# The front of an encoder layer: modulation quarters, norms and two weight tiles interleaved part by part

## What is computed

```python
mod = silu(c) @ w_mod + b_mod                      # shift1, scale1, gate1, shift2, scale2, gate2
h = rms_norm(x, g_mix) * (1 + scale1) + shift1
z = h @ w_in                                       # u_f | u_r | u_g
y_f = fourier_mixer(u_f, w_fourier)
y_r = bidirectional_rglru(conv(u_r), ...) * gelu(u_g)
x = x + gate1 * (concat(y_f, y_r) @ w_out)
x = x + gate2 * (square(relu(h2 @ w_ff1)) @ w_ff2)  # h2 from x as h above, with shift2, scale2
return rms_norm(x, g_final)
```

## Time and profile before

| | us |
|---|---|
| median of 3 runs | 1533.9 |
| the three runs | 1526.1, 1533.9, 1630.98 |
| the profiled execution, as timed | 1533.22 |
| its span in the trace | 1531.4 |
| PE busy in that span | 1433.7 |
| n = 5 (end of weight tile 1) done | 107.07 |
| n = 35 (end of the weight tiles) done | about 325.6 |

### The profile page before, as it was taken

One profiled execution on the slowest core, in us unless ns is written; L12 is line 12 of the kernel. 1 busy time (PEld: TensorE's weight loads), 2 busy tenths in 40 slices (PEclk: granted clock), 3 DMA queues, 4 the chain that ended last, 5 costly groups with the idle time before them and its releaser, 6 DMA issues.

```text
span 1531.4 us, 18516 instructions
## 1 busy us (share of the span) xinstructions
PE 1433.7 (94%) x7584; PEld 1203.2 (79%) x7584; DVE 830.9 (54%) x766; ACT 572.9 (37%) x664; POOL 558.4 (36%) x308
## 2 busy tenths in 40 slices
PE   3899999999899758999999999998999999999995
PEld 1467777788688548888888888887888888888884
DVE  6747778764344995534543443462565343344554
ACT  5447878445232342222232232232232322333230
POOL 5431212117200886454545545542232232232220
PEclk9899999999999888999999999999999999999997
DMA  9232322202512113332343333349998443445532
GB/s 381 98 118 102 143 88 73 83 9 78 189 55 83 48 49 124 132 148 110 121 165 114 121 151 121 117 167 388 386 382 308 162 181 138 145 189 203 193 124 83
DMA packets 74515, 232.35 MB, mean 152 GB/s; under 512 B 5568, under 2 KB 9792, under 8 KB 65728
## 3 DMA queue, kind: packets, MB, share of 16 engines
q1 hardware_dynamic: 74432, 231.17, 40.6%
HBM read 166.14 MB, written 65.01 MB: 151 GB/s over the span
## 4 chain that ended last, share of the span: by engine, by line
PE 58%; DVE 3%; DMA 1%; issue 1%; ACT 0%; SPq 0%; DVEq 0%; ACTq 0%
PE bank L887 19%; PE bank L888 19%; PE bank L889 19%; DMA hin<-hid_all 1%; DVE hin_lo L1876 0%; DVE x L1916 0%; DVE hid L1840 0%; DMA w_raw<-in_w_ff 0%; PE bank L946 0%; PE bank L939 0%; DVE fin_acc L1900 0%; DVE t4b_s L1774 0%; DVE lo_r L1782 0%; ACT hin_hi L1363 0%; DVE hid L1850 0%
## 5 line engine op out<-in xcount | busy, mean ns | idle before, releaser
L887 PE MATMUL bank<-hin_hi,w_lo 128*128 128x256 f32 (+1 forms) x896 | 303.1, 338 | 4.3 <-DVE hin_lo L1876 4.3
L888 PE MATMUL bank<-hin_lo,w_hi 128*128 128x256 f32 (+1 forms) x896 | 302.8, 338 | 0.0
L889 PE MATMUL bank<-hin_hi,w_hi 128*128 128x256 f32 (+1 forms) x896 | 302.2, 337 | 0.0
L1876 DVE TENSOR_TENSOR hin_lo<-hin,hin_hi 128x3072 fp32r<-128x3072 f32 x28 | 140.4, 5016 | 214.6 <-ACT hin_hi L1363 214.6
L2095 POOL TENSOR_TENSOR w_lo<-w_raw,w_hi 128x2048 fp32r<-128x2048 f32 x28 | 130.9, 4674 | 335.8 <-ACT w_hi L1351 334.3
L887 PEld LDWEIGHTS bank<-hin_hi,w_lo 128*128 128x128 f32 x896 | 170.9, 191 | 23.1 <-issue 4.7
L889 PEld LDWEIGHTS bank<-hin_hi,w_hi 128*128 128x128 f32 x896 | 170.6, 190 | 18.2
L888 PEld LDWEIGHTS bank<-hin_lo,w_hi 128*128 128x128 f32 x896 | 170.9, 191 | 17.6
L1351 ACT ACTIVATE w_hi<-w_raw 128x2048 fp32r<-128x2048 f32 x28 | 53.7, 1917 | 297.5 <-PE bank L889 175.8
L887 PE MATMUL bank<-t_hi,w_lo 128*128 128x512 f32 (+1 forms) x320 | 114.1, 357 | 14.5 <-ACT hid L1308 11.7
L1308 ACT ACTIVATE hid<-bank 128x768 f32<-128x768 f32 (+2 forms) x68 | 52.6, 773 | 182.8 <-PE bank L889 173.9
(11 more groups left out here) (258 smaller groups left out, 3270.2 us busy)
## 6 DMA issues: line engine op xcount, KB each, us to landing
hin<-hid_all SPq DMA_DIRECT2D x28, 1536.0 KB, 6.6
hid_all<-hid SPq DMA_DIRECT2D x105, 384.0 KB, 2.3
w_raw<-in_w_ff SPq DMA_DIRECT2D x36, 1024.0 KB, 9.0
w_raw<-in_w_ff SPq DMA_DIRECT2D x68, 256.0 KB, 2.9
mod_raw<-in_w_mod SPq DMA_DIRECT2D x16, 1024.0 KB, 6.5
x<-in_xT SPq DMA_DIRECT2D x6, 2048.0 KB, 13.1
mod_first<-in_w_mod SPq DMA_DIRECT2D x4, 2048.0 KB, 21.6
w_sums<-w_raw SPq DMA_DIRECT2D x8, 1024.0 KB, 14.4
```

The lines of the kernel that those rows point to most:

```text
L887: pe.matmul(out, w_lo, v_hi, start=first, stop=False, skip_group_check=True)
L888: pe.matmul(out, w_hi, v_lo, start=False, stop=False, skip_group_check=True)
L889: return pe.matmul(out, w_hi, v_hi, start=False, stop=last, skip_group_check=True)
L1876: dve.tensor_tensor(hin_lo[n % 3][:].rearrange("p t n -> p (t n)"), hin[n % 3][:].rearrange("p t n -> p (t n)"), hin_hi[n % 3][:].rearrang ...
```

## The change

The front is written out part by part. A part (c, q) is column group c with the row tiles 2q and 2q + 1; `FRONT` lists the twelve. In each part PE multiplies **both** weight tiles 0 and 1, into six banks. The norms of c = 1 and 2 and the quarters 1 to 3 are placed between parts. The loads go in that order too: x in six halves, weight tile 0, quarter 0 (in four pieces), x of c = 1, weight tile 1 into a raw buffer of its own, quarter 1, and so on. Weight tile 2 gets a third pair of split buffers.

The split operations are others: DVE multiplies x by amp1 and by an SBUF copy of the reciprocal root in one instruction, ACT writes `hi` = x + shift straight out, and DVE writes `lo` = (x + shift) - hi. POOL has only squares and weight splits left in the front. All three norms share bank 4 and one diagonal. The chain of small DVE operations for the decay stands behind the first `rstd`.

Behind the front, the gates move by two n (after n = 7, 8, 9, 10 and so on), and the `mod_step`s come singly after n = 5 to 20. Seven semaphores of the token splits become one, with counts in ACT's order of issue.

```diff
     sq8 = place("sq8", [P, KD, CH], F32, W0)
-    sq8_other = place("sq8_other", [P, KD, CH], F32, A0 + 16384)
+    sq8_other = place("sq8_other", [P, KD, CH], F32, A0 + 32768)
     diag_first = place("diag_first", [P, CH], F32, W0 + 16384)
-    rstd_sb = place("rstd_sb", [P, CH], F32, W0 + 18432)
+    rstd_sb = [place(f"rstd_sb{c}", [P, CH], F32, W0 + 18432 + 2048 * c) for c in range(NCH)]
 
     NQ = 4
...
+
+    FRONT = ((0, 0), (1, 0), (0, 1), (1, 1), (2, 0), (2, 1), (0, 2), (1, 2), (2, 2), (0, 3), (1, 3), (2, 3))
+
+    def in_bank(n):
+        return bank[(0, 1, 2, 3, 5, 4)[n] if n < 2 * NCH else n % 4]
+
+    def in_order(n):
+        j, c = divmod(n, NCH)
+        return 2 * c + j + 1 if j < 2 else n + 1
+
+    def win_of(j):
+        return 2 if j == 2 else j % 2
+
     def gates_after(j, c):
 
 
-        f, r = divmod(NCH * j + c - (2 * NCH - 1), 2 * NCH)
+        f, r = divmod(NCH * j + c - (2 * NCH + 1), 2 * NCH)
         return (2 * f + r // 2, r % 2) if 0 <= f < FT and r < 4 else None
 
-    def mod_steps_after(j):
-
-        return range(KD + 2 * j, KD + 2 * j + 2) if j < KD else ()
+    def mod_step_after(n):
+
+        s = n - (2 * NCH - 1) + KD
+        return s if KD <= s < 3 * KD else 0
 
     LRU_ALL = 2 * FT
...
@@ -473,14 +490,33 @@
     @block.sync
     def _(sp):
         sp.dma_start(vec[:], vec_d).then_inc(ld_vec, 16)
-        for c in range(NCH):
-            sp.dma_start(x[:, c, :, :], xT_d[:, c * CH:(c + 1) * CH].rearrange("(k p) n -> p k n", p=P)
-                         ).then_inc(ld_x[c], 16)
+
+        def load_x(c):
+            for h, s in enumerate((ld_x[c], ld_x2[c])):
+                rows = xT_d[h * FT * P:(h + 1) * FT * P, c * CH:(c + 1) * CH]
+                sp.dma_start(x[:, c, h * FT:(h + 1) * FT, :], rows.rearrange("(k p) n -> p k n", p=P)
+                             ).then_inc(s, 16)
+
+        def load_first(q):
+            src = w_mod1_d[q].rearrange("p (i k n) -> p i k n", i=2, k=KD)
+            parts = len(ld_first[q])
+            for h in range(parts):
+                ks = slice(h * KD // parts, (h + 1) * KD // parts)
+                for i in range(2):
+                    sp.dma_start(mod_first[q][:, i, ks, :], src[:, i, ks, :]).then_inc(ld_first[q][h], 16)
+
+        load_x(0)
         sp.dma_start(win_raw[:], w_in_d[TILES[0]]).then_inc(ld_win, 16)
+        load_first(0)
+        load_x(1)
+        sp.dma_start(win_raw1[:], w_in_d[TILES[1]]).then_inc(ld_wg, 16)
+        load_first(1)
+        load_x(2)
+        load_first(2)
+        load_first(3)
         sp.dma_start(dft_head[:], dft_head_d).then_inc(ld_dft, 16)
-
-        for q in range(NQ):
-            sp.dma_start(mod_first[q][:].rearrange("p i k n -> p (i k n)"), w_mod1_d[q]).then_inc(ld_first[q], 16)
+        sp.wait_ge(win_lo_done, 1)
+        sp.dma_start(win_raw[:], w_in_d[TILES[2]]).then_inc(ld_win, 16)
 
         def load_mod(s):
...
                          ).then_inc(ld_mod[s % 2], 16)
 
+        sp.wait_ge(win_lo_done, 2)
         sp.dma_start(wg_raw[:], w_gate_d[0]).then_inc(ld_wg, 16)
-        for j in range(NTILE):
-            if j + 1 < NTILE:
-                sp.wait_ge(win_lo_done, j + 1)
-                sp.dma_start(win_raw[:], w_in_d[TILES[j + 1]]).then_inc(ld_win, 16)
-            for s in mod_steps_after(j):
-                load_mod(s)
+        for j in range(1, NTILE):
+            if 2 < j + 1 < NTILE:
+                if j > 1:
+                    sp.wait_ge(win_lo_done, j + 1)
+                    sp.dma_start(win_raw[:], w_in_d[TILES[j + 1]]).then_inc(ld_win, 16)
+            for n in range(NCH * j, NCH * j + NCH):
+                if mod_step_after(n):
+                    load_mod(mod_step_after(n))
             if j % 2 == 1 and j // 2 + 1 < FT:
                 f = j // 2 + 1
...
@@ -682,8 +723,9 @@
         def mod_quarter(q):
 
             after(pe, mod_rows, q)
-            pe.wait_ge(ld_first[q], 16)
             for k in range(KD):
+                if k * len(ld_first[q]) % KD == 0:
+                    pe.wait_ge(ld_first[q][k * len(ld_first[q]) // KD], 32)
                 g = 32 * (k % 4)
                 m = pe.matmul(bank[MB][g:g + 32, :], c_silu[:, k, :], mod_first[q][:, :, k, :],
...
@@ -698,13 +740,17 @@
                               start=True, stop=True)
             m.then_inc(mod_tr, 1)
 
-        def first_tile(q):
-
-            pe.wait_ge(win_lo_done, 1)
-            for c in range(NCH):
+        def front(c, q):
+
+            i = FRONT.index((c, q))
+            for j in range(2):
+                if q == 0:
+                    pe.wait_ge(win_lo_done, j + 1)
+                if (c, q, j) == (2, 0, 1):
+                    pe.wait_ge(rstd_copied, NN)
                 for k in (2 * q, 2 * q + 1):
-                    pe.wait_ge((hlo_done, hlo_done_p)[k % 2], q * NCH + c + 1)
-                    m = three(bank[c][:], win_hi[0][:, k, :], win_lo[0][:, k, :], hi(c, k), lo(c, k),
+                    pe.wait_ge(hlo_done, 2 * i + k % 2 + 1)
+                    m = three(in_bank(NCH * j + c)[:], win_hi[j][:, k, :], win_lo[j][:, k, :], hi(c, k), lo(c, k),
...
@@ -734,8 +777,7 @@
             pe.wait_ge(wg_lo_done, f + 1)
             pe.wait_ge(conv_done, f + 1)
             if g == 0:
-                pe.wait_ge(xn_done, xn_count(NN))
-                pe.wait_ge(rstd_copied, 1)
+                pe.wait_ge(in_evac, 2 * NCH)
             pe.wait_ge(mod_cols, NQ if g < LRU_ALL // 2 else NQ + 1)
             for c in range(NCH):
...
         norm_sum(0)
         norm_spread(0)
+        pe.wait_ge(vec_dve, 2)
+        mod_quarter(0)
+        mod_quarter_sum(0)
+        front(0, 0)
         norm_sum(1)
         norm_spread(1)
+        mod_quarter(1)
+        front(1, 0)
+        mod_quarter_sum(1)
         norm_sum(2)
-        pe.wait_ge(silu_c, 1)
-        mod_quarter(0)
+        front(0, 1)
         norm_spread(2)
-        mod_quarter_sum(0)
-        for q in range(1, NQ - 1):
-            mod_quarter(q)
-            mod_quarter_sum(q)
-        mod_quarter(NQ - 1)
-        first_tile(0)
-        mod_quarter_sum(NQ - 1)
-        for q in range(1, NQ):
-            first_tile(q)
-
-        for j in range(NTILE):
+        front(1, 1)
+        mod_quarter(2)
+        front(2, 0)
+        mod_quarter_sum(2)
+        front(2, 1)
+        mod_quarter(3)
+        front(0, 2)
+        mod_quarter_sum(3)
+        for c, q in FRONT[7:]:
+            front(c, q)
+
+        for j in range(1, NTILE):
             for c in range(NCH):
-                if j > 0:
+                if j > 1:
                     in_tile(j, c)
                 if gates_after(j, c):
                     gates(*gates_after(j, c))
                 if (j, c) in MOD_AFTER:
                     mod_transpose(MOD_AFTER[j, c])
-            for s in mod_steps_after(j):
-                mod_step(s)
+                if mod_step_after(NCH * j + c):
+                    mod_step(mod_step_after(NCH * j + c))
             if j == AB_AFTER:
 
...
         def split_win_hi(j):
-            act.wait_ge(ld_win, 16 * (j + 1))
-            if j >= 2:
-                act.wait_ge(in_mm, NCH * (j - 1))
-            act.activation(win_hi[j % 2][:].rearrange("p k m -> p (k m)"), win_raw[:], ACT.Copy
...
+                act.wait_ge(ld_win, 16 * max(j, 1))
+            if j == 2:
+                act.wait_ge(norm_mm, NN)
+            elif j > 2:
+                act.wait_ge(in_mm, NCH * max(2, j - 1))
+            raw = win_raw1 if j == 1 else win_raw
+            act.activation(win_hi[win_of(j)][:].rearrange("p k m -> p (k m)"), raw[:], ACT.Copy
                            ).then_inc(win_hi_done, 1)
...
-        for n in range(NN):
-            for k in range(KD):
-                square(n, k)
-                if n > 0 and k == 3:
-                    root(n - 1)
-        act.wait_ge(norm_bc, 2)
-        act.activation(rstd_sb[:], norm_bank(1)[:], ACT.Copy).then_inc(rstd_copied, 1)
...
-
-            act.wait_ge(mod_cols, q + 1)
-            act.wait_ge(amp_set, q + 1)
-            for c, k in ((c, k) for c in range(NCH) for k in (2 * q, 2 * q + 1)):
-                s = SEQ_OF[c]
-                if c == 1:
-                    act.wait_ge(xn_done_p, KD)
-                else:
...
-                act.activation(x[:, c, k, :], x[:, c, k, :], ACT.Identity, bias=mod[:, SHIFT1, k, s:s + 1],
-                               scale=amp1[:, k, s:s + 1]).then_inc(h_done, 1)
-
-        root(NN - 1)
+        def copy_rstd(n):
+
+            act.wait_ge(norm_bc, n + 1)
+            act.activation(rstd_sb[n][:], norm_bank(n)[:], ACT.Copy).then_inc(rstd_copied, 1)
+
+        def front_hi(c, q):
+
+            s = SEQ_OF[c]
+            i = FRONT.index((c, q))
+            for k in (2 * q, 2 * q + 1):
+                act.wait_ge(xn_done, 2 * i + k % 2 + 1)
+                act.activation(hi(c, k), x[:, c, k, :], ACT.Identity, bias=mod[:, SHIFT1, k, s:s + 1]
+                               ).then_inc(hhi_done, 1)
+
```

(103 more changed lines are left out.)

122 lines of the change are left out of this document (48 added, 74 removed).

## The result

The kernel with the change takes 1555.4 us (median of four runs, 1551.9 to 1559.9) against 1530.2 for the kernel before (median of four, of which one is a slow execution of 1631.0 that the ratio leaves out). The ratio is 1.018, with an interval of 1.0133 to 1.0226: slower beyond doubt, but whether by more than 2% is not settled. The forecast was 1535, at most 1547, so the change costs some 25 us where 1 was expected. The profiled execution took 1552.1 as timed; its span is 1550.3, that is 18.9 above the span of before.

What follows compares the result with a forecast made beforehand. PE was taken as full except for 36 us of idle up to 90 us, bound by a chain of short steps between four engines. Front +0.55 and gates +0.65 gave +1.2 us: 1534.4 profiled, median 1535, range 1520 to 1547.

Steps and rivals of the forecast that it cites:

- The failed step: Behind the front: single `mod_step`s 6.5 us apart don't wait for `mod_raw`, as 1 MB lands in 2.5 us: 0.
- Gates after n = 25: Behind the front: the 2.5 us spare before these gates becomes between +0.5 and -1.3; taken as +0.65 us.
- The recurrence: End of the weight tiles: recurrence two n later, its tail ends at 325.0 against PE's last weight-tile matmul at 325.7: 0.
- The front's chain: Span start to end of tile 1: steps passing between four engines end at 105.7 against 105.15 before, +0.55 us.
- upper bound of 16.7: First norm, adds of squares: done at 13.0 if POOL is never in the way, 16.7 if fully; 14.8 taken.
- The four places where PE was to stand still: Front, 62.9 to 90.1: PE waits while copies, columns and splits pass through ACT's and DVE's lists.
- the clock: Front: PE's steps priced slow until about 52 us and fast from there; a part costs 5.2 or 2.8 us.
- PE stays slow: Rival, front: PE's clock stays low, five parts at 5.2 instead of 2.8 cost 12 us: 1547; chance 0.11.
- POOL's hold: Front: DVE operations reading SBUF twice wait for POOL, 0 to 2.36 us per weight split; half taken.
- The 38 for the end of part (0,0): Front: PE's part (0,0) needs POOL's weight split, forecast at 33.8, and ends about 38, ahead of the second norm's sum.
- the rivals of the front and the recurrence: Interleave pays: 1525 or 1519, chance 0.25; PE's clock stays slow: 1547, 0.11; recurrence late: at most 1546, 0.12.

Runs made afterwards that it cites:

- e1: The changed kernel with two `mod_raw` loads moved ahead of the wait for `wg_lo` in SP's list: 1540.5 us, ratio 1.007 to the kernel before.
- e6: The changed kernel with loads early, quarters 2 and 3 taken out of the chain of parts, and `mod_step`s in pairs again: 1523.4 us, ratio 0.9944 to before.
- e10: The kernel before with only the change's part behind the front, but `mod_step`s in pairs and their loads early: 1527.1 us, ratio 0.9997 to before.
- e5: The changed kernel with `mod_raw` loads early and 56 unread 128x128 matmuls added in the front's PE gaps: 1537.7 us, ratio 1.0047 to before.

## Why the prediction was wrong, step by step

**The failed step** is the sentence "The loads of `mod_raw` are waited for by single steps 6.5 us apart and 1 MB lands at the front's rates in 2.5: 0", and with it "PE is full to 326, so moved gates cost only if they stall it". It compared a rate with a rate, where the question was the moment of issue. The code shows what moved. The loads for an even tile stand behind the same `wg_lo` wait as before, but the first of them is now used after the tile's first n and not after its third, and the wait is released two n later, with the gates. The trace of before has the slack that was given up: a pair was issued a whole tile ahead, for two buffers. The 2.5 was wrong as well: it is 1 MB at the front's rate, while the page of before has, as the median from issue to landing,

```profile
mod_raw<-in_w_mod SPq DMA_DIRECT2D x16, 1024.0 KB, 6.5
```

and the late load of 164.51 took 7.6. The prediction followed the moved work through the lists of PE, ACT and DVE, and not through SP's. Two waits of 5.85 and 4.34 us, a third of 0.6, and slow stretches of PE's clock at the end of the two long ones (6.8 us from 170.3 and 3.4 from 228.3; what PE does in them takes twice as long) make 15 of the 19.1 (239.1 - 224.4, e1). The other 4.4 are the next two points.

**Gates after n = 25.** Forecast +0.65 within +0.5 to -1.3 of spare. It stalls in the place and for the reason forecast: the split of `uc` starts at 280.72, and PE's next gates at 282.58, 1.4 us after the last matmul's modelled end, where it had had 2.5 us to spare.

```profile
280.72 1.76 DVE L1660 TENSOR_TENSOR uc_lo<-uc,uc_hi 128x1536 fp32r<-128x1536 f32 x1
282.58 0.48 PE L690 MATMUL bank<-uc_hi,wg_lo 128*128 128x512 f32 x1 [1.41 <-issue]
```

The profile names no releaser for this wait; that it is the split rests on its end at 282.48, 0.1 ahead of the gates. Counted from where the next matmul could have started (280.77 + 0.23) the stall is 1.6, where 0.65 was taken and 1.3 was the bound: the mechanism was right, the size was not.

**Pairs made single.** Not in the sum at all; about 2.7 us by the rows (e6 and e10 remove it together with the stall).

**The recurrence.** "That just fits: 0" was right: behind n = 35 PE has the 0.7 for `u_f` and 0.6 for `pq_lo`, as in the kernel before, and e10 shows the delay to be free.

**The front's chain.** Forecast 105.7, measured 110.1. Up to part (2,0) each link is within 0.9 us, but for the first norm's sum, which is at its upper bound of 16.7; from there it falls behind:

| step | forecast | measured |
|---|---|---|
| first norm's sum starts on PE | 14.8 | 16.8 |
| columns of quarter 0 done | 27.0 | 27.9 |
| second norm's sum done | 39.9 | 40.2 |
| quarter 1 done | 47.0 | 47.3 |
| part (1,1) starts | 62.9 | 62.7 |
| part (2,0) starts | 69.8 | 70.1 |
| part (2,1) starts | 76.5 | 78.3 |
| part (0,2) starts | 83.4 | 86.8 |
| part (1,2) starts | 90.1 | 93.4 |
| tile 1 done | 105.7 | 110.1 |

The four places where PE was to stand still are there, waiting for what was named:

```profile
70.12 0.47 PE L690 MATMUL bank<-hi_f,win_lo 128*128 128x512 f32 x1 [2.20 <-DVE lo_f L1602]
78.28 0.80 PE L690 MATMUL bank<-hi_f,win_lo 128*128 128x512 f32 x1 [2.79 <-DVE lo_f L1602]
86.77 0.50 PE L690 MATMUL bank<-hi_r,win_lo 128*128 128x512 f32 x1 [2.11 <-DVE lo_r L1602]
93.41 0.80 PE L690 MATMUL bank<-hi_r,win_lo 128*128 128x512 f32 x1 [2.79 <-DVE lo_r L1602]
```

Two terms were mis-sized. The first is the clock: fast prices were taken from 52 on, but slow stretches of 6.8, 3.4, 3.4 and 6.8 us begin at 54.2, 71.3, 78.1 and 91.8, and the rows that start with 0.80 are in them. e5 prices them at some 2 us, not the 12 of the rival "PE stays slow". The second is POOL's hold, for which half was taken: it was there in full at the first norm, and DVE was held again at 28.0, 32.8 and 93.9.

```profile
10.70 5.92 DVE L1532 TENSOR_TENSOR sq<-sq 128x512 f32<-128x512 f32 x4 [7.21 <-ACT sq L1052]
93.94 3.53 DVE L1598 SCALAR_TENSOR_TENSOR x<-x,amp,rstd_sb 128x512 f32<-128x512 f32 x2
```

Four adds in 5.92 us, where alone they take 4 x 0.69, and two products in 3.53 against 1.41 alone. In the chain this costs 2 us at the first norm, and 2.1 at 93.9, where the sum had 1.2 for a weight split. That the 2 us are nearly gone by the second norm is luck: the forecast took slow prices for quarter 0 and its sum (3.64 and 1.87), but the clock rose at 23.5 and they took 2.60 and 1.05, 1.9 us less. The 38 for the end of part (0,0) is luck as well: the forecast's own terms give 33.8 and half a part at the slow price, 2.6, so 36.4, and 38.5 was met because POOL's split of weight tile 1 ended at 35.7. With e5's 2 that is 3 of the 4.4; the remaining 1 to 2 are not settled.

**The range.** It ended at 1547, built from the rivals of the front and the recurrence. No case held a wait for a load behind the front, so its 15 us had no chance at all; that is a missing case, not a narrow range.
